# Moving conditioning sums, one copy of normed rows and two gain stores to other quarters in a fused two-block transformer kernel

## The chip, the cores and the metric
The kernel runs as one program on one core of a Trainium2 chip. The metric is the device time of one execution in microseconds (us); the median of three executions of the kernel before is 2072.92 us. Engines are named as in the profile: PE is the matrix engine, DVE and ACT the vector and scalar engines, POOL and SP issue transfers (POOL also copies a little). SP does nothing but issue the weight loads.

## What is computed
Two blocks, one after the other, each on 256 rows of width 1024, all in fp32.

```python
# first block (one layer)
h = h + concat(rms(dilated_attention(...)), rms(moba_attention(...))) @ w_out
h = h + memory_cross_attention(rms(h), rms(mem), w_q_mem, w_kv_mem, w_o_mem)
h = h + conv_ffn(rms(h), w_gate, w_up, conv_w, conv_b, w_down)
# second block, two layers l, streams x and ctx (the context stream only in l = 0)
mod = silu(c) @ ada_w[l] + ada_b[l]          # 6 x 1024 values for x
modc = silu(c_ctx) @ ada_w[l] + ada_b[l]     # 6 x 1024 values for the context
p = (rms(x) * (1 + sc1) + sh1) @ w_in[l]     # q, k, v, gu, gv, conv, gates
y = (ga * (attn @ w_attn_o) + gg * (gmlp @ w_gmlp_o) + gc * (conv @ w_conv_o)) @ w_out[l]
x = x + g1 * rms(y)
x = x + g2 * rms(square(relu(modulate(rms(x), sh2, sc2) @ w_ff1[l])) @ w_ff2[l])
```

The products `silu(c) @ ada_w` are the "conditioning sums": a row times a matrix, done on DVE.

## The kernel before, in words
**Jobs and quarters.** The matrix work is cut into 162 jobs, J0 to J161, each a product of 256 rows with 512 columns of a weight matrix. A job has four quarters ("units"), written J9.2 for quarter 2 of J9. In program order: J0 to J19 are attention and memory attention of the first block (J6 to J8 and J13 weights of the memory's keys and values, J9 to J12 `w_out`, J16 to J19 the output product of the memory attention), J20 to J37 its feed-forward; J38 to J62 the mixer of layer 0 for the context stream, J63 to J87 the same for x (25 jobs later, same order); J88 to J119 the feed-forwards of layer 0; J120 the context's keys and values of layer 1, J121 to J145 its mixer, J146 to J161 its feed-forward. Within the mixer of the context, J38 and J39 are the first half of the conv input, J40 keys and values, J41 and J42 queries, J43 and J44 conv input, J45 to J48 the gmlp inputs, J49 to J58 gates with the attention's and gmlp's output products between (J51, J52 and J55, J56), J59 and J60 the conv's output product, J61 and J62 the last product. The layer norm of the conv sits on J56 to J58.

**How a quarter is done.** SP loads the 512 KB of raw weights into a ring `raw` of 5 buffers (L804); load n is issued once item n-5 of the ring's stream is used up, in order (L793 to L798). ACT copies raw to a rounded `whi` (`split`, L1586) once the load has landed and PE has used the same quarter of the job before. DVE subtracts, giving `wlo` (L2118), and PE does three products per tile (L1189 to L1191, or L1196 to L1198 where the weights move) as soon as `wlo` is there.

**Everything else hangs on quarters.** A function `make_plan` puts steps on a quarter of a job with `put(job, quarter, kind)`. ACT, DVE, PE, POOL and SP each run the steps of their own list strictly in the order of the quarters, so a step that waits holds up all that is behind it on its engine. There is no scheduler: the order is the table and the calls of `put`.

**Conditioning sums.** `COND_AT` (L36 to L38) names one place for each of 96 tiles of `ada_w`: (job, quarter, later), where later = 1 puts it behind the split. At the place DVE runs L1731 over a 128x1024 tile that came through the same ring (load `raw<-ada_wT`, L802) and adds it up to one column of `modc`. For all 48 tiles of layer 0 and the first 16 of layer 1 a second sum, for the context, runs straight behind on the same buffer; such a place is called a pair here.

**Mod steps.** `mod(job, quarter, layer, part, streams)` finishes a part of the modulation. Its "mix gain" part is, for each stream, two small DVE operations on 128x8 (L1820, L1828) and then, on POOL, a store `grow_dram<-modc` (L875) of 4 KB, whose elements of 4 bytes lie apart, with a wait for it before POOL goes on:

```python
pool.dma_start(dst, modc[:, MODS[p.l, p.s], p.first_r:p.units_done],
               allow_slow_non_contiguous=True).then_inc(sem["grow_st"], 16)
pool.wait_ge(sem["grow_st"], 16 * p.k)
```

POOL later loads the gain back as rows (`GB<-grow_dram`, L814).

**Normed rows.** `ynS`, `ynM`, `ynL` make the normed and transposed attention outputs for `w_out` in two halves: `ynM` on DVE is a reciprocal square root (L1785, L1642 to L1649) and a product (L1790), `ynL` copies the result to a rounded high part on ACT (L1340) and a low part on DVE (L1796). Its second half stands on J8.3, the last quarter of a job of the memory's values; J9 and J10 need only the first half, J11 and J12 the second.

Of the kernel before, what the change touches and what calls it, by code (L numbers as in the profile page):

```python
# [32 lines left out]
ON_DVE = ((0, 1, 2), (4, 5))  # L33
RING, LEAD = 5, 2
C2W = 60
COND_AT = (((2, 3, 0), (3, 3, 1), (4, 3, 1), (5, 2, 0), (6, 3, 0), (7, 3, 0), (8, 2, 0), (9, 3, 1), (13, 3, 1), (14, 2, 1), (15, 2, 1), (16, 1, 1), (17, 0, 1), (19, 0, 0), (20, 2, 1), (22, 2, 1), (24, 2, 1), (26, 2, 1), (28, 1, 1), (29, 1, 1), (30, 2, 1), (34, 1, 1), (35, 0, 1), (36, 2, 0), (38, 1, 1), (39, 2, 1), (40, 2, 1), (42, 3, 0), (43, 3, 1), (44, 2, 1), (45, 3, 0), (53, 1, 0), (54, 1, 0), (55, 1, 0), (56, 2, 0), (61, 3, 0), (63, 3, 0), (64, 2, 1), (68, 3, 0), (69, 3, 0), (70, 3, 0), (72, 1, 0), (73, 3, 0), (75, 0, 1), (76, 0, 1), (78, 1, 0), (79, 1, 0), (80, 1, 0)),  # L36
           ((85, 1, 1), (87, 1, 0), (88, 3, 1), (91, 1, 0), (92, 0, 0), (93, 0, 0), (94, 1, 1), (95, 1, 1), (96, 0, 0), (97, 0, 0), (98, 1, 1), (99, 1, 1), (100, 0, 0), (101, 0, 0), (102, 1, 1), (103, 1, 1)),
           ((105, 0, 0), (106, 0, 0), (107, 0, 0), (108, 2, 0), (109, 1, 0), (110, 0, 0), (111, 0, 0), (112, 2, 0), (113, 1, 0), (114, 0, 0), (115, 0, 0), (116, 0, 0), (117, 0, 0), (118, 0, 0), (118, 3, 0), (119, 2, 0), (121, 0, 0), (121, 3, 0), (122, 3, 0), (123, 3, 0), (126, 1, 0), (127, 0, 0), (127, 3, 0), (128, 3, 0), (129, 3, 0), (130, 3, 0), (131, 3, 0), (133, 1, 0), (134, 1, 0), (136, 1, 0), (137, 1, 0), (138, 1, 0)))  # L38
EPS = 1e-6
NEG = -1e30  # L40
MAGIC = 1597463007.0
# [73 lines left out]
def make_plan():  # L115
# [3 lines left out]
    def job(evac, w, n0, typ, slot, k0=0, nk=KT, n=NW, ready=None, **args):  # L119
        units = {8: [[0, 1], [2, 3], [4, 5], [6, 7]], 6: [[0, 1], [2, 3], [4], [5]],  # L120
                 "low": [[0], [1], [2], [3]], "high": [[4], [5], [6], [7]]}[nk]
        jb = Step("job", evac=evac, w=w, n0=n0, typ=typ, slot=slot, k0=k0, nk=nk, cols=n, units=units,
                             ready=ready or {}, aux=[[], [], [], []], **args)
        jobs.append(jb)
        return jb

    def put(jb, q, kind, **args):
        p = Step(kind, **args)
        jb.aux[q].append(p)
        return p  # L130
# [38 lines left out]
    j_vm0 = job("cp", "w_kv", 1024, "A", 1, ready=um, dst=("cres", 0))  # L169
# [14 lines left out]
        put(hosts[2], 1, "ynS", half=group)  # L184
        put(hosts[2], 2, "ynM", half=group)
    put(j_km0, 1, "ynL", slot=2, half=0)
    put(j_vm0, 3, "ynL", slot=2, half=1)
    y_ready = {0: [("yn_lo", None, 0, 1)], 2: [("yn_lo", None, 0, 2)]}
    j_oa = [job("res", "w_out", n * NW, "A", 2, nk="low", ready={0: y_ready[0]}, res="x") for n in range(2)]
    j_ob = [job("res", "w_out", n * NW, "A", 2, nk="high", ready={0: y_ready[2]}, res="x") for n in range(2)]  # L190
    j_vm1 = job("cp", "w_kv", 1536, "A", 1, ready=um, dst=("cres", 1))

    def half_squares(jb, wait_job):
# [50 lines left out]
    def mod(jb, q, l, part, *streams):  # L244

        for s in streams:
            put(jb, q, "mod", l=l, s=s, part=part)
# [196 lines left out]
    t_next = prenorm(d1[1], 2, d2[0], 2, 0, "c", 0, "RA", 0, [("ctx_in", None, 0, 16), ("cp_done", j_q0, 1, 1)])  # L444
    put(d2[1], 1, "gb", src=("g_final",))
    J, co, wo = mixer(0, "c", t_next, (0, 1, 2))
    mod(J["gu0"], 0, 0, "mix gain", "c", "x")

    fin = Step("final", after={"act": [("res_done", d2[1], 1, 1)], "dve": [("res_done", d2[1], 1, 1)]})
    J["ga0"].aux[2].insert(0, fin)  # L450
# [7 lines left out]
    J, _, wo = mixer(0, "x", t_next, (2, 1, 0), tab, first=first)  # L458
# [24 lines left out]
    J, _, wo = mixer(1, "x", t_next, (1, 0, 2), tab, kvc)  # L483
# [12 lines left out]

    places = [at for part in COND_AT for at in part]
    assert places == sorted(places) and len(places) == LAYERS * 6 * KT
# [161 lines left out]

def build(nc, A, out):
    jobs, tail, stream = make_plan()
    with ExitStack() as ctx:
        def tiles3(ap):
# [1537 lines left out]
```

## Time and profile before

| | |
|---|---|
| three executions | 2072.63, 2072.92, 2073.53 us, median 2072.92 |
| the profiled execution | 2073.14 us, span in the profile 2071.3 us |
| granted PE clock, mean | 0.991 of 2.4 GHz |
| busy: PE, DVE, ACT, POOL | 1982.4, 1679.1, 1113.7, 111.5 us |
| what the DMA engines moved | 404.65 MB |

The span is from the first to the last instruction that the profiler saw; the device time is 1.8 us longer. Times inside the trace are counted from the start of the span. An entry of the timeline gives the start, the duration, the engine, the line, what it writes and reads and, in brackets, how long the engine sat idle before it and what ended that. PE is idle for 89 us of the span in all, 17 of them at the start and about 33 at three norms that nothing covers (J19, J145, J161).

### The profile page before, as it was taken

How to read it: one execution, taken by the hardware profiler on the slowest of the kernel's cores; microseconds unless marked ns; L12 is line 12 of the kernel's file. 1: busy time of each engine (PE TensorE's matmuls, PEld its weight loads, DVE VectorE, ACT ScalarE, POOL GpSimd, SP SyncE). 2: the span in 40 equal slices, each digit the busy share in tenths (PEclk: the TensorE clock that was granted, in tenths of full speed). 3: DMA queues.
4: the chain of work that ended last, by engine and by line, in shares of the span. 5: the costliest groups of instructions: out<-in, count | busy, mean ns of one | idle time of the engine just before them, and what ended most of it. 6: DMA issues, size and time to landing. Idle time of an engine off the chain costs nothing.

```text
span 2071.3 us, 29703 instructions
## 1 busy us (share of the span) xinstructions
PE 1982.4 (96%) x11317; PEld 1692.7 (82%) x11317; DVE 1679.1 (81%) x2616; ACT 1113.7 (54%) x1529; POOL 111.5 (5%) x217
## 2 busy tenths in 40 slices
PE   7999979999989999999999999999999999998998
PEld 6877879989878778888777888888888887787886
DVE  5888678888978987988988888977888889876665
ACT  5555444455574365566436654554665664365553
POOL 3000000000004000001300000000000013000000
PEclk9999989999999999999999999999999999999999
DMA  8546466667666655655656667777666566654653
GB/s 264 191 125 205 157 205 204 193 206 250 195 140 202 205 185 191 193 153 177 206 170 192 211 218 247 238 244 239 229 221 197 154 192 204 193 176 130 210 179 121
DMA packets 196718, 404.65 MB, mean 195 GB/s; under 512 B 15815, under 2 KB 18067, under 8 KB 196576
## 3 DMA queue, kind: packets, MB, share of 16 engines
q1 hardware_dynamic: 187888, 387.50, 59.9%
q0 software_dynamic: 8688, 15.25, 2.5%
q8 instruction: 91, 1.49, 0.3%
q14 instruction: 51, 0.42, 0.1%
HBM read 396.74 MB, written 1.10 MB: 192 GB/s over the span
## 4 chain that ended last, share of the span: by engine, by line
PE 73%; DVE 13%; ACT 7%; issue 4%; DMA 2%; DVEq 0%; ACTq 0%
PE gps L1189 13%; PE gps L1191 13%; PE gps L1190 13%; PE gps L1213 8%; PE gps L1196 5%; PE gps L1198 5%; PE gps L1197 5%; PE gps L1215 4%; DVE wlo L2118 3%; ACT whi L1586 2%; PE aps L1125 2%; PE gps L1173 2%; DVE Yc L1934 2%; PE aps L971 1%; PE aps L1097 1%
## 5 line engine op out<-in xcount | busy, mean ns | idle before, releaser
L2118 DVE TENSOR_TENSOR wlo<-raw,whi 128x1024 fp32r<-128x1024 f32 (+1 forms) x648 | 760.2, 1185 | 248.8 <-ACT whi L1586 246.2
L1586 ACT ACTIVATE whi<-raw 128x1024 fp32r<-128x1024 f32 (+1 forms) x648 | 660.4, 1027 | 538.0 <-PE gps L1191 376.8
L1189 PE MATMUL gps<-whi,both 128*128 128x512 f32 x1624 | 649.1, 400 | 9.5 <-DVE wlo L2118 9.5
L1191 PE MATMUL gps<-whi,both 128*128 128x512 f32 x1624 | 634.2, 391 | 0.0
L1190 PE MATMUL gps<-wlo,both 128*128 128x512 f32 x1624 | 633.9, 390 | 0.0
L1189 PEld LDWEIGHTS gps<-whi,both 128*128 128x128 f32 x1624 | 305.8, 188 | 82.7 <-DVE wlo L2118 14.8
L1191 PEld LDWEIGHTS gps<-whi,both 128*128 128x128 f32 x1624 | 305.4, 188 | 65.5
L1190 PEld LDWEIGHTS gps<-wlo,both 128*128 128x128 f32 x1624 | 306.0, 188 | 60.8
L1196 PE MATMUL gps<-both,whi 128*128 128x256 f32 x960 | 276.0, 288 | 2.5 <-DVE wlo L2118 2.5
L1197 PE MATMUL gps<-both,whi 128*128 128x256 f32 x960 | 271.5, 283 | 0.0
L1198 PE MATMUL gps<-both,wlo 128*128 128x256 f32 x960 | 271.5, 283 | 0.0
L1213 PE MATMUL gps<-both,whi 128*128 128x512 f32 x672 | 238.0, 399 | 0.3 <-DVE wlo L2118 0.3
L1731 DVE SCALAR_TENSOR_TENSOR junk<-raw,cond_rows 128x1024 uint8<-128x1024 f32 x160 | 195.1, 1219 | 4.3 <-DMA raw<-ada_wT 3.2
L1196 PEld LDWEIGHTS gps<-both,whi 128*128 128x128 f32 x960 | 183.9, 192 | 8.1 <-issue 4.3
L1934 DVE SCALAR_TENSOR_TENSOR Yc<-GLP,CW,Yc 128x256 f32<-128x256 f32 x450 | 189.0, 478 | 0.0
L1215 PE MATMUL gps<-both,wlo 128*128 128x256 f32 x672 | 188.7, 281 | 0.0
L1197 PEld LDWEIGHTS gps<-both,whi 128*128 128x128 f32 x960 | 184.0, 192 | 0.6
L1198 PEld LDWEIGHTS gps<-both,wlo 128*128 128x128 f32 x960 | 184.0, 192 | 0.0
L1213 PEld LDWEIGHTS gps<-both,whi 128*128 128x128 f32 x672 | 126.3, 188 | 31.9 <-DVE wlo L2118 0.6
L1215 PEld LDWEIGHTS gps<-both,wlo 128*128 128x128 f32 x672 | 127.0, 189 | 0.3
L917 POOL DMA_DIRECT2D QP<-GLP x144 | 70.4, 498 | 77.4 <-PE aps L1073 34.4
L1529 ACT ACTIVATE TT<-gps 128x512 f32<-128x512 f32 x42 | 25.1, 598 | 70.9 <-PE gps L1215 70.9
(306 smaller groups left out, 1746.3 us busy)
## 6 DMA issues: line engine op xcount, KB each, us to landing
raw<-w_in SPq DMA_DIRECT2D x232, 512.0 KB, 4.3
raw<-w_ff SPq DMA_DIRECT2D x192, 512.0 KB, 4.6
raw<-ada_wT SPq DMA_DIRECT2D x96, 512.0 KB, 4.4
raw<-w_attn_o SPq DMA_DIRECT2D x24, 512.0 KB, 4.3
raw<-w_gmlp_o SPq DMA_DIRECT2D x24, 512.0 KB, 4.0
raw<-w_conv_o SPq DMA_DIRECT2D x24, 512.0 KB, 4.3
raw<-w_out SPq DMA_DIRECT2D x24, 512.0 KB, 4.7
raw<-w_gate SPq DMA_DIRECT2D x20, 512.0 KB, 4.6
```

The source lines that it names most:

```text
L1189: mm(om, ah, whi[:, q, i, :], start=first, stop=False)
L1190: mm(om, ah, wlo[:, q, i, :], start=False, stop=False)
L1191: t = mm(om, al, whi[:, q, i, :], start=False, stop=last)
L1196: mm(on, wh, ohi[:, jb.slot, k, :], start=first and n % 2 == 0, stop=False, skip_group_check=True)
L1197: mm(on, wh, olo[:, jb.slot, k, :], start=False, stop=False, skip_group_check=True)
L1198: t = mm(on, wl, ohi[:, jb.slot, k, :], start=False, stop=last, skip_group_check=True)
L1213: mm(tiles(o[:, n * NW:(n + 1) * NW], 2), whi[:, q, i, c], both[:, :, jb.slot, k, :], start=first, stop=False, skip_group_check=True)
L1215: t = mm(o[:, n * NW:n * NW + S], wlo[:, q, i, c], ohi[:, jb.slot, k, :], start=False, stop=last, skip_group_check=True)
L1586: A_(part(whi, jb, q), raw_part(jb, q), ACT.Copy).then_inc(hi_done[q], 1)
L1731: stt(junk[:, :], raw[:, a.at % RING].rearrange("p a n -> p (a n)"), 0.5, CB[:, p.v, :], ALU.mult, ALU.mult, accum_out=modc[:, i, p.r:p.r ...
L1934: stt(y, x, CW[:, p.l, tap * KT + k:tap * KT + k + 1], y, ALU.mult, ALU.add).then_inc(sem["cv_done"], 1)
L2118: tt(part(wlo, jb, q), raw_part(jb, q), f32(part(whi, jb, q)), ALU.subtract).then_inc(lo_done[q], 1)
```

## The change
Three things move; nothing is added or removed in number (96 tiles of sums, one copy, two stores, as before).

1. **Conditioning sums.** `COND_AT` has other places. Taken out (job, quarter, later): (9,3,1), (13,3,1), (14,2,1), (15,2,1), (16,1,1), (17,0,1), (19,0,0), (29,1,1), (36,2,0), (40,2,1), (44,2,1), (45,3,0), (53,1,0), (54,1,0), (55,1,0), (56,2,0), (61,3,0), (78,1,0), (79,1,0), (80,1,0), (85,1,1), (112,2,0), (113,1,0), (122,3,0), (123,3,0), (136,1,0), (137,1,0), (138,1,0). Put in: (14,0,1), (14,3,0), (15,3,0), (29,0,1), (29,3,1), (31,3,1), (40,1,1), (44,3,0), (46,1,0), (47,1,0), (48,3,0), (50,0,1), (50,3,0), (57,1,1), (58,0,1), (58,3,1), (61,0,1), (65,3,0), (71,2,1), (73,0,1), (90,1,0), (112,1,0), (113,0,0), (120,1,0), (122,2,0), (123,1,0), (124,1,0), (125,1,0). The tiles keep their order, so a tile is summed where the next place of the list stands.
2. **The second half of `ynL`** goes from J8.3 to J9.0.
3. **The mix gain of layer 0**, both streams, goes from J47.0 to J41.1.

```diff
@@ COND_AT, first lines of each part @@
-COND_AT = (((2, 3, 0), (3, 3, 1), (4, 3, 1), (5, 2, 0), (6, 3, 0), (7, 3, 0), (8, 2, 0), (9, 3, 1), (13, 3, 1), (14, 2, 1), (15, 2, 1), (16, 1, 1), (17, 0, 1), (19, 0, 0), (20, 2, 1),
...
+COND_AT = (((2, 3, 0), (3, 3, 1), (4, 3, 1), (5, 2, 0), (6, 3, 0), (7, 3, 0), (8, 2, 0), (14, 0, 1), (14, 3, 0), (15, 3, 0), (20, 2, 1),
...
     put(j_km0, 1, "ynL", slot=2, half=0)
-    put(j_vm0, 3, "ynL", slot=2, half=1)
     y_ready = {0: [("yn_lo", None, 0, 1)], 2: [("yn_lo", None, 0, 2)]}
     j_oa = [job("res", "w_out", n * NW, "A", 2, nk="low", ready={0: y_ready[0]}, res="x") for n in range(2)]
     j_ob = [job("res", "w_out", n * NW, "A", 2, nk="high", ready={0: y_ready[2]}, res="x") for n in range(2)]
+    put(j_oa[0], 0, "ynL", slot=2, half=1)
...
     J, co, wo = mixer(0, "c", t_next, (0, 1, 2))
-    mod(J["gu0"], 0, 0, "mix gain", "c", "x")
+    mod(J["q0"], 1, 0, "mix gain", "c", "x")
```

**What the change does to DVE's list at J8 and J9.** `both<-RB,both` is the low part of `ynL`, `wlo` the split of a quarter, `xres<-xres,gps` the evacuation of a job of `w_out`.

```order
 L1790 SCALAR_TENSOR_TENSOR RB<-RB,C,GB 128x256 x4
+L2118 TENSOR_TENSOR wlo<-raw,whi 128x512
 L1796 TENSOR_TENSOR both<-RB,both 128x1024
-L2118 TENSOR_TENSOR wlo<-raw,whi 128x512 x4
-L1731 SCALAR_TENSOR_TENSOR junk,modc<-raw,cond_rows 128x1024
-L1979 TENSOR_TENSOR xres<-xres,gps 128x2x512
-L2118 TENSOR_TENSOR wlo<-raw,whi 128x512
-L1731 SCALAR_TENSOR_TENSOR junk,modc<-raw,cond_rows 128x1024
 L2118 TENSOR_TENSOR wlo<-raw,whi 128x512 x3
```

One split now comes before the low part, and a conditioning sum (two operations) is gone from the quarters behind it.

**DVE's list at J41 and J42**, in the queries of the context; `AB` is the normed keys.

```order
 L1883 TENSOR_TENSOR AB<-AB,st 128x512
 L1851 TENSOR_TENSOR AB<-AB,GQK 128x256 x2
+L1820 TENSOR_TENSOR modc<-modc,ADB 128x8
+L1828 TENSOR_TENSOR modc<-modc,C 128x8
+L1820 TENSOR_TENSOR modc<-modc,ADB 128x8
+L1828 TENSOR_TENSOR modc<-modc,C 128x8
 L2118 TENSOR_TENSOR wlo<-raw,whi 128x1024
 L1934 SCALAR_TENSOR_TENSOR Yc<-GLP,CW,Yc 128x256 x3
```

The four small operations that release the two stores now stand behind the keys' norm, some 85 rows earlier than before.

**POOL's list at the same place.** `GB<-gmlp_norm_g` is a load of the gmlp's gain, `GQK<-k_norm_g` one of the keys' gain.

```order
 L814 DMA GQK<-k_norm_g 128x128
 L814 DMA QP<-gmlp_ws 128x4x128
+L875 DMA grow_dram<-modc 128x8x1 x2
 L814 DMA GB<-gmlp_norm_g 128x1024
-L875 DMA grow_dram<-modc 128x8x1 x2
 L814 DMA GB<-grow_dram 128x1024
```

The two stores pass a load on POOL's queue, which now goes out behind them.

## Rows read from the trace of the kernel before
**Rows 1.** The page: busy time of the engines, and the chain of waits.
```profile
PE 1982.4 (96%) x11317; PEld 1692.7 (82%) x11317; DVE 1679.1 (81%) x2616; ACT 1113.7 (54%) x1529; POOL 111.5 (5%) x217
...
PE 73%; DVE 13%; ACT 7%; issue 4%; DMA 2%; DVEq 0%; ACTq 0%
```
**Rows 2.** Timeline of PE: restarts after idle time, and three rows without one.
```profile
165.31 0.50 PE L1189 MATMUL gps<-whi,both 128*128 128x512 f32 x1 [3.61 <-DVE wlo L2118]
...
167.41 0.63 PE L1190 MATMUL gps<-wlo,both 128*128 128x512 f32 x1
...
463.48 0.50 PE L1189 MATMUL gps<-whi,both 128*128 128x512 f32 x1 [1.16 <-DVE wlo L2118]
...
530.02 1.03 PE L1075 MATMUL aps<-kvb,QP 128*128 128x256 f32 x4
...
617.50 1.10 PE L1097 MATMUL aps<-QP,kvb 128*128 128x256 f32 x4 [2.28 <-ACT QP L1402]
...
763.37 0.50 PE L1189 MATMUL gps<-whi,both 128*128 128x512 f32 x1 [0.82 <-DVE wlo L2118]
...
798.67 0.50 PE L1189 MATMUL gps<-whi,both 128*128 128x512 f32 x1 [1.41 <-DVE wlo L2118]
...
1067.07 1.36 PE L1135 MATMUL aps<-Yc,ones 128*32 128x256 f32 x16 [2.17 <-issue]
...
1127.62 1.09 PE L971 MATMUL aps<-ident,RA 128*128 128x128 f32 x8 [0.92 <-DVE RA L2008]
...
1588.03 0.39 PE L1196 MATMUL gps<-both,whi 128*128 128x256 f32 x1 [0.64 <-DVE wlo L2118]
```
**Rows 3.** Timeline of DVE: the splits behind the low part of `ynL`.
```profile
164.57 2.49 DVE L2118 TENSOR_TENSOR wlo<-raw,whi 128x512 fp32r<-128x512 f32 x4
```
**Rows 4.** Timeline of ACT: the copy at J8, and at J43, J44 and J49.
```profile
162.05 1.06 ACT L1340 ACTIVATE both<-RB 128x1024 fp32r<-128x1024 f32 x1 [6.41 <-DVE RB L1790]
...
525.42 2.16 ACT L1586 ACTIVATE whi<-raw 128x1024 fp32r<-128x1024 f32 x2
527.49 1.01 ACT L1369 ACTIVATE QP<-aps 128x1024 f32<-128x1024 f32 x1
...
615.81 1.06 ACT L1586 ACTIVATE whi<-raw 128x1024 fp32r<-128x1024 f32 x1 [2.11 <-DMA raw<-w_in]
```
**Rows 5.** The page, groups of instructions: the conditioning sums.
```profile
L1731 DVE SCALAR_TENSOR_TENSOR junk<-raw,cond_rows 128x1024 uint8<-128x1024 f32 x160 | 195.1, 1219 | 4.3 <-DMA raw<-ada_wT 3.2
```
**Rows 6.** Busy time per stretch: start, end, length, each engine, PE clock, DMA share, GB/s.
```profile
588.00:618.00 30.00, 25.88 (x116) 20.49 (x115) 22.44 (x42) 19.49 (x34) 2.36 (x3) 1.00 0.68 108
...
592.00:595.00 3.00, 3.00 (x15) 2.47 (x14) 1.25 (x2) 3.00 (x7) 0.00 (x0) 1.00 0.42 17
...
604.00:607.00 3.00, 3.00 (x15) 2.49 (x14) 2.81 (x6) 1.25 (x5) 0.00 (x0) 1.00 1.03 382
...
736.00:764.00 28.00, 26.86 (x117) 21.38 (x116) 22.94 (x35) 21.78 (x28) 1.44 (x2) 1.00 0.49 156
```
**Rows 7.** The store's line, all six of the kernel, min/median/max.
```profile
DMA to landing us min/median/max: 10.3/10.9/13.9
```
**Rows 8.** Timeline of POOL at J47 to J50.
```profile
591.00 0.91 POOL L875 DMA_DIRECT2D grow_dram<-modc  x1 [107.56 <-DVE modc L1828]
601.73 0.89 POOL L875 DMA_DIRECT2D grow_dram<-modc  x1 [9.82 <-DMA grow_dram<-modc]
```
**Rows 9.** DMA issues: whole span; 591.5 to 602; 1080 to 1097. KB each, us to landing.
```profile
raw<-w_in SPq DMA_DIRECT2D x232, 512.0 KB, 4.3
...
raw<-w_in SPq DMA_DIRECT2D x4, 512.0 KB, 14.4
...
raw<-w_conv_o SPq DMA_DIRECT2D x5, 512.0 KB, 12.9
```
**Rows 10.** Timeline of DVE at J41: the row behind which the stores' operations stand.
```profile
510.89 0.76 DVE L1851 TENSOR_TENSOR AB<-AB,GQK 128x256 f32<-128x256 f32 x2
```
**Rows 11.** Timeline of SP: one weight load between the two stores' issues.
```profile
596.65 0.37 SPq L804 DMA_DIRECT2D raw<-w_in  x1
```

More of the change, by code:

```diff
@@ L35 @@
 C2W = 60
-COND_AT = (((2, 3, 0), (3, 3, 1), (4, 3, 1), (5, 2, 0), (6, 3, 0), (7, 3, 0), (8, 2, 0), (9, 3, 1), (13, 3, 1), (14, 2, 1), (15, 2, 1), (16, 1, 1), (17, 0, 1), (19, 0, 0), (20, 2, 1), (22, 2, 1), (24, 2, 1), (26, 2, 1), (28, 1, 1), (29, 1, 1), (30, 2, 1), (34, 1, 1), (35, 0, 1), (36, 2, 0), (38, 1, 1), (39, 2, 1), (40, 2, 1), (42, 3, 0), (43, 3, 1), (44, 2, 1), (45, 3, 0), (53, 1, 0), (54, 1, 0), (55, 1, 0), (56, 2, 0), (61, 3, 0), (63, 3, 0), (64, 2, 1), (68, 3, 0), (69, 3, 0), (70, 3, 0), (72, 1, 0), (73, 3, 0), (75, 0, 1), (76, 0, 1), (78, 1, 0), (79, 1, 0), (80, 1, 0)),
-           ((85, 1, 1), (87, 1, 0), (88, 3, 1), (91, 1, 0), (92, 0, 0), (93, 0, 0), (94, 1, 1), (95, 1, 1), (96, 0, 0), (97, 0, 0), (98, 1, 1), (99, 1, 1), (100, 0, 0), (101, 0, 0), (102, 1, 1), (103, 1, 1)),
-           ((105, 0, 0), (106, 0, 0), (107, 0, 0), (108, 2, 0), (109, 1, 0), (110, 0, 0), (111, 0, 0), (112, 2, 0), (113, 1, 0), (114, 0, 0), (115, 0, 0), (116, 0, 0), (117, 0, 0), (118, 0, 0), (118, 3, 0), (119, 2, 0), (121, 0, 0), (121, 3, 0), (122, 3, 0), (123, 3, 0), (126, 1, 0), (127, 0, 0), (127, 3, 0), (128, 3, 0), (129, 3, 0), (130, 3, 0), (131, 3, 0), (133, 1, 0), (134, 1, 0), (136, 1, 0), (137, 1, 0), (138, 1, 0)))
@@ new lines @@
+COND_AT = (((2, 3, 0), (3, 3, 1), (4, 3, 1), (5, 2, 0), (6, 3, 0), (7, 3, 0), (8, 2, 0), (14, 0, 1), (14, 3, 0), (15, 3, 0), (20, 2, 1), (22, 2, 1), (24, 2, 1), (26, 2, 1), (28, 1, 1), (29, 0, 1), (29, 3, 1), (30, 2, 1), (31, 3, 1), (34, 1, 1), (35, 0, 1), (38, 1, 1), (39, 2, 1), (40, 1, 1), (42, 3, 0), (43, 3, 1), (44, 3, 0), (46, 1, 0), (47, 1, 0), (48, 3, 0), (50, 0, 1), (50, 3, 0), (57, 1, 1), (58, 0, 1), (58, 3, 1), (61, 0, 1), (63, 3, 0), (64, 2, 1), (65, 3, 0), (68, 3, 0), (69, 3, 0), (70, 3, 0), (71, 2, 1), (72, 1, 0), (73, 0, 1), (73, 3, 0), (75, 0, 1), (76, 0, 1)),
+           ((87, 1, 0), (88, 3, 1), (90, 1, 0), (91, 1, 0), (92, 0, 0), (93, 0, 0), (94, 1, 1), (95, 1, 1), (96, 0, 0), (97, 0, 0), (98, 1, 1), (99, 1, 1), (100, 0, 0), (101, 0, 0), (102, 1, 1), (103, 1, 1)),
+           ((105, 0, 0), (106, 0, 0), (107, 0, 0), (108, 2, 0), (109, 1, 0), (110, 0, 0), (111, 0, 0), (112, 1, 0), (113, 0, 0), (114, 0, 0), (115, 0, 0), (116, 0, 0), (117, 0, 0), (118, 0, 0), (118, 3, 0), (119, 2, 0), (120, 1, 0), (121, 0, 0), (121, 3, 0), (122, 2, 0), (123, 1, 0), (124, 1, 0), (125, 1, 0), (126, 1, 0), (127, 0, 0), (127, 3, 0), (128, 3, 0), (129, 3, 0), (130, 3, 0), (131, 3, 0), (133, 1, 0), (134, 1, 0)))
```

## The prediction
> **What bounds the kernel.** I read the page first: PE is busy 96% of the span and carries 73% of the chain of waits, DVE 13%, ACT 7% [rows 1]. So PE is the bound, and a change of order can only win or lose in the 89 us in which PE is idle, or in stretches at half clock. Then I went through PE's timeline for its restarts [rows 2]; the brackets say what ended each idle time, mostly DVE's `wlo` or an ACT copy that DVE or a load held up. Then the stretches [rows 6], for how much of DVE is free where sums come or go, and at last the transfers [rows 7 to 9], since each step that moves takes its DMA along.
>
> A sum is 1219 ns of DVE [rows 5], with its small accumulator read 1.25 us; a pair is 2.5 us. Where DVE is ahead of PE, a pair costs and gives nothing.
>
> **The copy of normed rows.** Before, DVE waits for ACT's copy (162.05, 1.06 us), does the low part and then splits at 164.57 [rows 3, 4]; PE restarts at 165.31, 0.74 us behind the split's start, after 3.61 us [rows 2]. With one split ahead of the copy DVE can split at 162.0, when its product is done, and PE restarts near 162.7. That quarter takes PE 1.36 us; the next split stands behind the copy (about 164.4), so PE waits again until about 165.2. Before, PE reached this second quarter at 165.31 + 1.36 = 166.7: **-1.5 us**. Behind the long idle time PE's rows take 0.63 us at 167.41 where 0.39 is normal [rows 2]; that is the 1.2 GHz level, for 3.4 us, half of which is lost. With two shorter gaps in its place I expect it gone: **-1.6 us** (0 if it stays).
>
> **Sums taken out.** At J36.2 a pair stands right before the `wlo` that PE waits for: PE's 1.16 us at 463.48 [rows 2] go: **-1.2**. At J61.3 likewise, 1.41 us at 798.67 [rows 2]: **-1.4**. J85.1 pushes the row behind PE's 0.92 us at 1127.62 [rows 2]: **-0.9**. J53 to J56: DVE waits there for ACT, which waits for PE; **-0.4** at most. J78 to J80: the same **-0.4**, and 2.17 us of idle at 1067.07 [rows 2] are followed by a stretch at 1.2 GHz of the same length as above; slightly earlier work may save it, 0.8 x 1.6 = **-1.3**. J16 to J19: **-0.2**. J9, J13, J29, J45, J136 to J138: DVE is idle beside them, so 0 (cover: the lead of `wlo` over PE; without it 2.5 us each). Together **-5.8**.
>
> **Sums put in.** J57 to J60: three pairs, 7.5 us, into a stretch where DVE is busy 22.94 of 28 us [rows 6], so 5.1 us are free; the rest is late, and PE already waits for `wlo` behind it at 763.37 [rows 2]: **+2.4**. J124 and J125: two single sums (2.5 us) ahead of splits for which PE already waits 0.64 us at 1588.03 [rows 2]: **+2.5**. J65.3, J71.2, J73.0: three pairs between the head norms and copies of x, of which I take a third, **+2.5** (0 to 7.5: DVE has free time there, but not in the norm itself). J61.0: **+0.6**. J31.3: **+0.4**. J48.3, J50.0, J50.3: **+0.5**. J120.1: **+0.2**. J14, J15, J40, J44, J46, J47, J90, J112, J113, J122, J123: 0, covered as above. Together **+9.1**.
>
> **The two stores.** This is the largest term, and the sums are not part of it. A store of 4 KB takes 10.3 to 13.9 us to land [rows 7]; the second goes out at 601.73, once the first has landed [rows 8], and is over some 13.9 us later. While the first is under way, the core moves 17 GB/s between 592 and 595; at 604 to 607 it is 382 [rows 6]. The four weight loads issued between 591.5 and 602 took 14.4 us, where a load takes 4.3; five at another pair of stores took 12.9 [rows 9]. So for some 25 us a weight load is late by 8 to 10 us. The Trainium skill ("DMA: Bandwidth & Descriptors", "Queues, rings and completion order") says that each DMA engine goes round between the queues it has work for, packet by packet; by that two stores of 4 KB would slow the loads by next to nothing, and the stores' term would be -2.0 us instead of what follows. Rows 6 and 9 speak against it.
>
> Before, the ring is full at this time; only one split is late, ACT's at 615.81 by 2.11 us [rows 4], and PE loses 2.28 us at 617.50 [rows 2]. That goes: **-2.0**. After, the stores' operations stand behind the row at 510.89 [rows 10], so the first goes out about 511.7 and the second about 522.4. The loads for J43.3 and J44.0 are issued within 8 us of the first. At J47 the load issued at 596.65 [rows 11], 5.65 us after the first store, is the one that ACT waited for until 615.81 [rows 4]: 24.8 us after the first store, just behind the second. The next one landed within a microsecond of it. Here that is 536 to 537. Their splits stand at 525.42 to 527.6 now [rows 4], and behind them in ACT's list is the copy of the queries at 527.49, for which PE's product at 530.02 waits [rows 2]. With the split at 537 the copy comes at 538 and PE at 539: **+9.0**, and 9 us of idle time bring the 1.2 GHz level, which at 167.41 cost up to 1.6: **+1.0**. Bounds: +1 if J44.0 is the only thing late and lands with the first two (14 to 16 us after the first store), +12 if the second store's 13.9 us apply. The load `GB<-gmlp_norm_g`, which the stores pass on POOL's queue, has 60 us left: 0. Together **+8.0**.
>
> **The sum.** -3.1 - 5.8 + 9.1 + 8.0 = +8.2 us. Against the profiled execution's 2073.14 (span 2071.3 and 1.8 around it; the median of the three is 0.2 lower) that is **2081.3 us**. Changes within 0.2% (4.1 us) can't be told from none here: faster is below 2068.8, slower above 2077.1.
>
> **Rivals.**
> - *The loads slip past the stores* (the other side). Place: J43.3 and J44.0; it decides whether these two loads land before about 527, ahead of the second store, as four of the five did at 1080 to 1097 (they were issued within 10.4 us of the first store and landed by 16.6 us after it). Then nothing is late at J43, and all the idle time of PE in 588 to 618, 30 - 25.88 = 4.1 us [rows 6], goes with the stores. The stores' term is -4.1 instead of +8.0: 2069.2 us. Against it: at J47 the same spacing of loads was caught. The skill's rule on the queues would lead here too. 0.28.
> - *The sums put in are absorbed.* DVE's free time at J57 to J60 and J65 to J73 lies where it is needed, and at J124 PE's lead takes it: 8.0 of the 9.1 us go: 2073.3 us. For it: DVE is free for 19% of the span [rows 1]. Against: the steps in front of these splits are chains, which can't be moved into the gaps. 0.16; with the first rival as well, 2061.2: 0.08.
> - *The copy does not do what it says.* ACT, not DVE, sets J9: the evacuation moved ahead of the copy waits for PE, so the copy is late and J11 waits for it. The 3.1 us stay: 2084.4. 0.05.
>
> **How the numbers follow.** Forecast 0.43, the rivals 0.28, 0.16, 0.08 and 0.05. Around each stand some 3 us for the unknown sizes. Slower by over 0.2%: most of the forecast, the last rival and a little of the third: 0.45. Faster by over 0.2%: half of the first rival, the double case and a little: 0.25. Within: 0.30. The range leaves out the double case and the upper end of the stores' bound: 2066 to 2085; the forecast's own is 2077 to 2085.
>
> **What the profile after would show.** Stores of L875 near 512 and 523; ACT's split near 537 after 8 to 9 us of waiting for `raw<-w_in`; PE's L1075 restarting near 537 after some 9 us; no 2.28 us at J49; PE near 162.7 at J9 and no row of 0.63 us behind; DVE without a gap from 736 to 764 and PE waiting 2 us more there and at J126. I am wrong if ACT waits under 2 us at J43 and J44, or if PE's idle times at J60, J68 and J126 are as before.

## The result and the profile after

The changed kernel takes 2085.02 us (median of four executions, 2081.78 to 2086.65) where the kernel before took 2072.78 beside it (2072.24 to 2073.53). The ratio is 1.0056, 95% interval 1.0044 to 1.0069: 9 to 14 us slower. The profiled execution is the longest of the four (2086.65 us, span 2084.8, mean PE clock 0.985 against 0.991); the shortest, 2081.78, ran at a mean clock of 0.990. Of the executions below, one of `mods_only` that took 4011 us is left out of every number.

The page of the changed kernel, to be set against [rows 1]:

```profile
span 2084.8 us, 29701 instructions
...
PE 1991.6 (96%) x11317; PEld 1700.3 (82%) x11317; DVE 1678.5 (81%) x2616; ACT 1114.3 (53%) x1529; POOL 111.7 (5%) x217
...
PE 71%; DVE 15%; ACT 7%; issue 4%; DMA 2%; DVEq 0%; ACTq 0%
```

The same matmuls are busy 9 us longer (1991.6 against 1982.4), and PE is idle 93 us against 89. So in these two executions only about a third of the difference is waiting; the rest is work at the lower clock level (1.2 GHz), which by the mean clocks lasts some 63 us in all against 37. Not all of that belongs to the change, as shown further down.

PE's waits of the changed kernel, what it waited for, total, times, longest:

```profile
PE aps L971 <- DVE RB L1676: 19.8, 3, 10.0
...
PE aps L1075 <- ACT QP L1369: 8.7, 1, 8.7
PE gps L1189 <- DVE wlo L2118: 8.2, 11, 2.4
PE gps L1196 <- DVE wlo L2118: 4.7, 3, 2.4
```

The 8.7 us are new: before, this product ran at 530.02 without a wait [rows 2]. Timeline of POOL, then of ACT, then of PE in the changed kernel, at the mix gain's new place:

```profile
503.53 0.91 POOL L875 DMA_DIRECT2D grow_dram<-modc  x1 [257.23 <-DVE modc L1828]
514.71 0.89 POOL L875 DMA_DIRECT2D grow_dram<-modc  x1 [10.27 <-DMA grow_dram<-modc]
```
```profile
516.91 1.06 ACT L1586 ACTIVATE whi<-raw 128x1024 fp32r<-128x1024 f32 x1 [6.02 <-DMA raw<-w_in]
...
528.34 1.06 ACT L1586 ACTIVATE whi<-raw 128x1024 fp32r<-128x1024 f32 x1 [7.61 <-DMA raw<-w_in]
529.30 1.01 ACT L1369 ACTIVATE QP<-aps 128x1024 f32<-128x1024 f32 x1
```
```profile
530.45 2.05 PE L1075 MATMUL aps<-kvb,QP 128*128 128x256 f32 x4 [8.67 <-ACT QP L1369]
```

It reads as the forecast had it for J44.0: its load is in only at 528.34, 24.8 us after the first store was issued, ACT's split of it waits 7.6 us, the queries' copy stands behind the split, and PE stands 8.67 us. The load for J43.3 was not late with it: ACT splits it at 519.68, about 16 us after the first store, before the second can hold it up. The program is by then some 8 us ahead of the kernel before, so the times are earlier than forecast by that much.

Stretches of the changed kernel (columns as in [rows 6]); the clock is the third number from the end:

```profile
526.00:534.00 8.00, 3.55 (x12) 3.22 (x13) 3.94 (x6) 2.91 (x3) 0.56 (x1) 0.50 0.90 303
722.00:730.00 8.00, 7.72 (x38) 5.89 (x39) 3.37 (x4) 1.45 (x2) 0.00 (x0) 0.79 0.51 170
752.00:766.00 14.00, 11.12 (x41) 8.35 (x40) 11.46 (x13) 10.84 (x14) 0.00 (x0) 0.88 0.62 223
1598.00:1606.00 8.00, 6.51 (x35) 6.24 (x36) 6.75 (x9) 3.10 (x4) 0.00 (x0) 0.79 0.78 243
```

Behind the stall at J43 (until 535.9, and once more at 546 to 550), in the layer norm, at J59 and at J126 the clock is down for some microseconds; in the stretches that answer to these four the kernel before has a clock of 1.00. The fall in the layer norm can't be put down to the change, though: `copy_only` (0.58 over 718 to 722) and `j19_only` (0.57 over 720 to 724) below have it as well, and they leave the sums there and the stores alone.

The other places, PE's restarts of the changed kernel, against [rows 2]:

```profile
161.76 0.50 PE L1189 MATMUL gps<-whi,both 128*128 128x512 f32 x1 [0.97 <-DVE wlo L2118]
...
164.18 0.50 PE L1189 MATMUL gps<-whi,both 128*128 128x512 f32 x1 [0.77 <-DVE wlo L2118]
...
760.71 0.50 PE L1189 MATMUL gps<-whi,both 128*128 128x512 f32 x1 [2.37 <-DVE wlo L2118]
...
1127.13 1.09 PE L971 MATMUL aps<-ident,RA 128*128 128x128 f32 x8 [0.30 <-DVE RA L2008]
...
1599.49 0.38 PE L1196 MATMUL gps<-both,whi 128*128 128x256 f32 x1 [2.39 <-DVE wlo L2118]
```

The one wait of 3.61 us at J9 has become two of 0.97 and 0.77, and no matmul behind them takes 0.63 us. J59 has a wait of 2.37 us, J126 one of 2.39 where it was 0.64.

Where each quarter starts in the one and in the other tells where the difference of the two profiled executions (13.5 us at the end) comes from: -3.2 at J9 and J10, -2.9 at J20, -1.9 at J37, +12.9 at J43 and J44, -2.2 at J49, +1.0 at J51, +6.5 from J56 to J60, +0.7 and -1.8 at J61 and J62, +3.2 from J67 to J74, -1.8 at J85 and J86, +4.1 at J125 and J126 (the rest is in steps under 1 us).

### The profile page after: what moved, and what is told of

Read it like the earlier page. It is cut to its first block, busy times and chain, and to the rows that moved or that the text cites. A ratio compares the mean times of both kernels' runs of the same rounds, so it can differ in the third digit from the quotient of the medians.

```text
span 2084.8 us, 29701 instructions
## 1 busy us (share of the span) xinstructions
PE 1991.6 (96%) x11317; PEld 1700.3 (82%) x11317; DVE 1678.5 (81%) x2616; ACT 1114.3 (53%) x1529; POOL 111.7 (5%) x217
## 4 chain that ended last, share of the span: by engine, by line
PE 71%; DVE 15%; ACT 7%; issue 4%; DMA 2%; DVEq 0%; ACTq 0%
PE gps L1189 12%; PE gps L1191 12%; PE gps L1190 12%; PE gps L1213 8%; PE gps L1196 5%; PE gps L1198 5%; PE gps L1197 5%; DVE wlo L2118 4%; PE gps L1215 4%; ACT whi L1586 2%; DVE Yc L1934 2%; PE aps L1125 2%; PE gps L1173 1%; PE aps L971 1%; DVE junk L1731 1%
## 5 line engine op out<-in xcount | busy, mean ns | idle before, releaser
L1196 PEld LDWEIGHTS gps<-both,whi 128*128 128x128 f32 x960 | 186.7, 194 | 10.7 <-DVE wlo L2118 5.4
L1197 PEld LDWEIGHTS gps<-both,whi 128*128 128x128 f32 x960 | 186.7, 195 | 0.7
L1213 PEld LDWEIGHTS gps<-both,whi 128*128 128x128 f32 x672 | 126.3, 188 | 31.9 <-DVE wlo L2118 0.6
```

The source lines that it names most:

```text
L1196: mm(on, wh, ohi[:, jb.slot, k, :], start=first and n % 2 == 0, stop=False, skip_group_check=True)
L1197: mm(on, wh, olo[:, jb.slot, k, :], start=False, stop=False, skip_group_check=True)
L1213: mm(tiles(o[:, n * NW:(n + 1) * NW], 2), whi[:, q, i, c], both[:, :, jb.slot, k, :], start=first, stop=False, skip_group_check=True)
```

## The experiments

All ratios are to the kernel before, run on the same chip in the same rounds, with 95% intervals; a thousandth is 2.07 us. The difference of two ratios is uncertain by some 3 us. Each profile is of one execution.

### Are the stores the cause?

`mods_back`: the change, with the mix gain back.

```diff
-    mod(J["q0"], 1, 0, "mix gain", "c", "x")
+    mod(J["gu0"], 0, 0, "mix gain", "c", "x")
```

> The change with the mix gain of layer 0 back on J47.0, everything else as in the change. Theory (the two gain stores hold up the loads for J43.3 and J44.0): the 8.7 us that PE waits for the queries' copy and the half clock behind it go, the 2.2 us at J49 come back, so 2085.0 - 11 = about 2074 us. Rival (the sums and the copy make the loss, the stores only happen to sit there): it stays above 2082 us.

Measured: 1.0023 (1.0013 to 1.0034), median 2077.54: neither the 2074 of the theory nor the 2082 of the rival. So the stores' place is worth more than half of the loss, but not all: the sums and the copy are 4.8 us slower without it, which leads to the table of sums.

`mods_only`: the kernel before, with the mix gain alone moved.

```diff
-    mod(J["gu0"], 0, 0, "mix gain", "c", "x")
+    mod(J["q0"], 1, 0, "mix gain", "c", "x")
```

> The kernel before with the mix gain alone moved to J41.1. Theory of the stores: slower than before by 9 to 12 us, about 2083 us, with PE idle 8 to 9 us at J43 or J44 behind the copy of the queries. Rival (the stores hurt only because the changed kernel has less lead there, from the sums at J40 and J44): under 4 us slower, below 2077 us.

Measured: 1.0047 (1.0033 to 1.0061), 9.7 us slower (median of five 2083.74). PE's waits of this kernel have the same new row, and the rival (less lead through the moved sums) falls:

```profile
PE aps L1075 <- ACT QP L1369: 9.6, 1, 9.6
```

### One store or two?

`one_store`: the kernel before, the context's store early, the x stream's where it was.

```diff
+    mod(J["q0"], 1, 0, "mix gain", "c")
+    mod(J["gu0"], 0, 0, "mix gain", "x")
-    mod(J["gu0"], 0, 0, "mix gain", "c", "x")
```

> The kernel before with only the context's mix gain on J41.1 and the x stream's left on J47.0, so one store goes early. Theory (it is the second store, started as soon as the first has landed, that catches the loads of J43.3 and J44.0): these loads land about 5 us after the single store has, by 528, and PE waits under 3 us there: at most 3 us slower than before, and the stall at J49 of before gets smaller, so 2071 to 2076 us. Rival (one store is enough): half or more of the loss of the two, 2078 us or more.

Measured: 1.0023 (1.0013 to 1.0032), 4.8 us slower, median 2077.76: half of what the two cost, so nearly the rival's case and not the theory's. ACT and PE in this kernel (its lines are numbered one higher):

```profile
526.27 1.06 ACT L1587 ACTIVATE whi<-raw 128x1024 fp32r<-128x1024 f32 x1 [6.71 <-DMA raw<-w_in]
...
532.27 1.06 ACT L1587 ACTIVATE whi<-raw 128x1024 fp32r<-128x1024 f32 x1 [1.42 <-DMA raw<-w_in]
```
```profile
534.38 2.04 PE L1076 MATMUL aps<-kvb,QP 128*128 128x256 f32 x4 [3.94 <-ACT QP L1370]
```

One store holds back the loads for about 12 us; the splits then follow each other at the pace at which the loads land, not at ACT's, and PE waits 3.94 us, with the clock low until 540.3. I had put under 3 us on it, since I counted only one late load and not the queue of them. The second store makes up the other half: with it the same load is late by another store's time.

### Is it the 4 KB or the pieces?

`runs_32b`: the kernel before with the mix gain at J41.1, and the destination laid out in runs. The rows of the gain come out in another order by this, so the kernel computes something else; the work is the same.

```diff
-dst = grow_dram.ap()[...].rearrange("(r c) -> c r", c=P)
+dst = grow_dram.ap()[...].rearrange("(c r) -> c r", c=P)
```

> The kernel before with the mix gain moved to J41.1, and the store's destination laid out so that the 8 values of a partition lie together (runs of 32 bytes, 128 of them, where it was 1024 single values of 4 bytes); the gain rows are permuted by this, so the output is another. Theory (the count of scattered pieces is what takes the 10 us and holds up the loads, not the 4 KB): a store lands in about 2 to 3 us, the loads in their usual 4 to 5 us, no stall at J43, and the stall at J49 gone: 2069 to 2072 us. Rival (any store by POOL to memory in this place costs as much): landing 10 us and about 2083 us as with the scattered form.

Measured: 0.9984 (0.9974 to 0.9993), 3.3 us faster than before, median 2069.55. The store's line, all six of this kernel, against [rows 7]:

```profile
DMA to landing us min/median/max: 1.7/3.0/4.0
```

Same bytes, same place, same queue, 128 pieces for 1024: 3.0 us for 10.9, no stall at J43, and 13 us between this kernel and `mods_only` (0.9984 and 1.0047). So the cause is the scattered form, and the place only decides how much of it shows. In `runs_32b` J49 starts its second quarter 2.2 us earlier than before, and J85 and J86 some 2 us. Of these about half can't be put down to the stores: in `copy_only`, which keeps them as they were, the two places are 1.0 and 1.4 us earlier too. Whether a scattered store issued by another engine would do the same was not tried.

### The sums and the copy, each alone

`sums_only`: the kernel before with the changed `COND_AT`.

> The kernel before with the changed table of sums alone; the copy and the mix gain stay where they were. By the trace of the change the table gains 2.6 us at J20 (the pair at J19.0 gone), 1.9 at J37, 1.8 at J62, 1.8 at J85 and J86, and loses 5 to 6 at J58 to J60, 3 at J67 to J74, 4 at J125 and J126, 1 at J51 and 0.7 at J61. Theory (the table is a net loss): 5 to 8 us slower than before, 2078 to 2081 us. Rival (the places gain as much as they lose, as the sum of the prediction had it, +3.3): 2074 to 2077 us.

Measured: 1.0036 (1.0025 to 1.0047), 7.5 us slower, median 2081.18. The table is a net loss, twice as large as predicted. Some 4 us of it arise at J49 to J51, where the whole change loses 1.0. ACT and PE of `sums_only` there:

```profile
610.61 1.06 ACT L1586 ACTIVATE whi<-raw 128x1024 fp32r<-128x1024 f32 x1 [5.44 <-DMA raw<-w_in]
611.57 0.89 ACT L1394 ACTIVATE QP<-QP,den 128x256 f32<-128x256 f32 x2
```
```profile
612.61 1.09 PE L1084 MATMUL aps<-ident,QP 128*128 128x128 f32 x4 [5.06 <-ACT QP L1394]
```

In the kernel before, this product at 611.85 waits 1.65 us. It is the stores again, at their old place J47.0: with the added sums around them a late load meets a step that PE needs sooner, and the mean clock over 610 to 618 is 0.57. `mods_back` and `combined_slow` have the same (waits of 3.98 and 3.90 us); `combined_fast`, which has these sums and short stores at J47.0, has not (1.31 us). Which of the added sums does it was not tried.

`copy_only`: the kernel before with `put(j_oa[0], 0, "ynL", slot=2, half=1)` in place of `put(j_vm0, 3, ...)`.

> The kernel before with the second half of the copy moved to J9.0 and nothing else. Theory (one split ahead of the copy and no half clock behind a shorter wait): PE restarts near 162.7 and stays at full clock, 3 us faster, about 2069.5 us. Rival (the conditioning sum at J9.3, which this kernel keeps, or the clock takes it back): under 1.5 us faster.

Measured: 0.9989 (0.9978 to 0.9999), 2.3 us faster, median 2070.93, with PE's restarts at 162.02 and 164.45 and full clock behind. The low level behind J9's long wait is in each of the seven profiles that keep the copy at J8.3 and in none of the seven that have it at J9.0. J9 and J10 gain 3.2 us in this profile, but PE gives 1.2 back at 188.50, in a wait of 1.35 us for normed rows that neither the kernel before nor the changed one has. The three parts alone, 9.7 + 7.5 - 2.3 = 14.9 us, are some 4 us uncertain and so agree with the whole change's 9 to 14; they need not add up, since the loss at J49 in `sums_only` needs the stores at J47.0.

### Which sums?

`ln_sums_out`: `mods_back` with three pairs moved out of the layer norm's quarters. Not both sums of a place with later = 1 stand behind the split: `make_plan` puts the context's sum on the next quarter, and the first sum stays in front. So these three places are six single sums in front of six quarters, and a tile keeps its place in the ring until the second of them (737.15 and 746.46 in the profile of the change for J57.1). J53 to J55 are true pairs.

```diff
-(57, 1, 1), (58, 0, 1), (58, 3, 1),
+(53, 1, 0), (54, 1, 0), (55, 1, 0),
```

> The change with the mix gain back on J47.0 and the three pairs at J57.1, J58.0 and J58.3 back on J53.1, J54.1 and J55.1. Theory (these pairs stand in front of the layer norm's chain and of splits that have no lead, so nearly each of their 7.5 us shows): 5 us less than the same kernel with them (2077.5), about 2072.5 us, and PE's waits of 2.4 us at J59 gone. Rival (DVE's 5 us of free time there take them, as the prediction had it): 2 to 3 us less, 2075 us.

Measured: 0.9999 (0.9989 to 1.0008), against 1.0023 with them: 5.0 us for the three pairs, 2 to 8 by the intervals (median 2073.48). In the two profiles the quarters from J56 to J61 differ by 5.5 us. The stretch 744 to 772 of this kernel, and of the change, which is some 6 us behind it there:

```profile
744.00:772.00 28.00, 26.84 (x121) 21.45 (x120) 23.39 (x30) 20.04 (x26) 0.00 (x0) 1.00 0.63 204
```
```profile
744.00:772.00 28.00, 23.88 (x95) 18.27 (x93) 24.26 (x36) 19.98 (x26) 1.44 (x2) 0.94 0.46 161
```

DVE is free for more than 3 us in both, and PE does 3 us less of work in the second, with a part of the stretch at the lower clock. DVE's timeline of the change says why the free time does not help:

```profile
754.04 1.23 DVE L2118 TENSOR_TENSOR wlo<-raw,whi 128x1024 fp32r<-128x1024 f32 x1
757.03 1.22 DVE L1955 SCALAR_TENSOR_TENSOR RB<-RB,Yc 128x1024 f32<-128x1024 f32 x1 [1.76 <-ACT RB L1455]
758.17 1.22 DVE L1731 SCALAR_TENSOR_TENSOR junk<-raw,cond_rows 128x1024 uint8<-128x1024 f32 x1
```

DVE sits idle for 1.76 us in the layer norm, for ACT's tanh, and then has the sum to do before the split that PE waits for at 760.71. DVE's step and the split are both in order behind what came before: DVE's free time lies where ACT is late, and the sum where DVE is.

`j19_only`: the kernel before with one pair moved, `(19, 0, 0)` to `(15, 3, 0)`.

> The kernel before with the one pair at J19.0 put on J15.3 instead (the tiles between shift by a place). The prediction gave its removal nothing. Theory (DVE and the load of this pair stand in the chain of the norm at J19 and J20, which nothing covers; DVE waits 3.2 us for it at 259.3): PE's wait at the norm falls from 12.5 to about 10 us, 2 to 3 us faster than before, about 2070.5 us. Rival (nothing, as predicted: the norm is set by PE and ACT): within 1 us of before.

Measured: 0.9989 (0.9980 to 0.9999), 2.3 us faster (0.2 to 4.1), median 2071.98. In the profile the longest wait for the norm's rows falls only from 12.51 to 11.4 us. The prediction's "nothing" is wrong; how much it is for this pair alone, 1 or 2 us, stays open.

`combined_slow` and `combined_fast`: `ln_sums_out` with five more of the added sums back where they were, and, in the second, the short store with a result that is still the reference's.

```diff
-(65, 3, 0), (71, 2, 1), (73, 0, 1), (124, 1, 0), (125, 1, 0)
+(78, 1, 0), (79, 1, 0), (80, 1, 0), (136, 1, 0), (137, 1, 0)
```
```diff
+G = GB[:].rearrange("p (c r) -> p r c", r=D // P)[:, jb.j * NW // P:(jb.j + 1) * NW // P, :]
+rc = lambda t: t.rearrange("p (r c) -> p r c", c=P)
-tt(y[:, 1, j], src[:, 1, :], GB[:, j], ALU.mult)
+tt(rc(y[:, 1, j]), rc(src[:, 1, :]), G, ALU.mult)
... (the other three products likewise)
```

> The combined table, copy and place of the mix gain, with the scattered stores as in the kernel before. Against the same with ln_sums alone moved back (2073.3) it tells what the sums at J65.3, J71.2, J73.0, J124.1 and J125.1 cost: theory 3 + 3 to 4 us, so 2067 us; rival (PE's lead had absorbed them): 2071 us or more. Against the combined kernel with short stores (2065.5) it tells what these give: 2 to 4 us.

> What the runs so far favour, put together: the change's copy and the sums it takes out at J9 to J19, J36, J61 and J85; the sums that it puts in at J57, J58, J65, J71, J73, J124 and J125 at J53 to J55, J78 to J80, J136 and J137 instead, as before; the mix gain on J47.0; and the store in runs of 32 bytes, with the gain's rows read through a strided view so that the result is that of the reference. Theory (each cause is local, so the terms add): 2077.5 - 5 (J57, J58) - 3 (J65 to J73) - 3 (J124, J125) - 3 (stores) = about 2063.5 us, faster than both kernels. Rival (the gains run into each other, or the strided view costs DVE time at the two gained evacuations): 2068 us or more.

Measured: 0.9969 (0.9957 to 0.9981), median 2067.08, and 0.9962 (0.9949 to 0.9976), median 2066.24. Both beat both kernels, by 6 and 8 us against before. Against `ln_sums_out` the five places (three pairs, two single sums, 10 us of DVE) cost 0.9999 - 0.9969, 6.2 us; in the profiles it is 3.0 at J65 to J74 and 3.3 at J124 to J126. The short store with its view gave 1 us on top, which is within the noise; 2 to 4 were expected. In the profiles it gives 3.8 us at J49 and loses most of it again further on.

`fast_store`: the kernel before with only that store and view. `after_fast`: the whole change with them.

> The kernel before with the gain stores in runs of 32 bytes and the strided view of the gain's rows, all else in place, the output as the reference's. Theory: a store lands in about 3 us; PE's 2.3 us at J49 go and some 2 us at J85 and J86, so 3 to 4 us faster than before, about 2069.5 us. Rival (the strided view costs what the stores give): within 1 us of before.

> The whole change, mix gain on J41.1, but with the stores in runs of 32 bytes. Theory (the place of the stores is harmless once they are short, and the sums and the copy stay as they are): the change's 2084.5 less 11.5 for the stall and less some 1.5 at J85, about 2073 us, no stall at J43. Rival (at J41 any store or the load behind it on POOL's queue does harm): 2077 us or more.

Measured: `fast_store` 1.0013 (1.0003 to 1.0022), 2.7 us slower than before, outside the theory and the rival; `after_fast` 1.0006 (0.9996 to 1.0015), median 2074.9, near the 2073 expected, with no stall at J43. The stores land in 2.8 and 3.1 us (medians), so they did their part. In the profile of `fast_store` the quarters behind J49 and J86 are 2.8 us ahead of before, and all of it is lost again by J121. What most likely took it back is the view. The gained evacuation (L2054 before, L2056 here) in `fast_store`, then in the kernel before:

```profile
L2056 DVE TENSOR_TENSOR RB<-gps,GB 128x512 f32<-128x512 f32 x6 | 6.7, 1111 | 0.9 <-PE gps L1191 0.9
```
```profile
L2054 DVE TENSOR_TENSOR RB<-gps,GB 128x512 f32<-128x512 f32 x6 | 4.1, 689 | 0.9 <-PE gps L1191 0.9
```

Reading one operand with a step of 32 bytes takes 1111 ns for 689. There are 24 of these, 10 us of DVE in all, and they stand in the chains ahead of the norms: between `runs_32b`, which has the same store and no view, and `fast_store` lie 6 us (0.9984 and 1.0013). The two differ also in the mix gain's place, so the view alone is not isolated. A version that reads the rows in one run and still stores in runs was not tried.

## Why the prediction was right, and where it was not

The forecast was 2081.3 us (+8.2), the measurement 2085.0 (+12.2 to the median, 9 to 14 by the ratio). That is at the very top of the stated range of 2066 to 2085. Direction, place and mechanism of the largest term held; the table of sums was put at under half of what it cost, so the range held the result only at its edge.

- **The two stores, +8.0.** Right in mechanism: the row that ACT waits for, the copy behind it, PE's product behind that, 24.8 us from the first store to the late load, as at J47, 8.67 us of idle time for the 9.0 forecast. `mods_only` gives 9.7 us. Mis-sized was the clock behind the stall: I put 1.0 us. In the profile PE works at 1.2 GHz from 530.45 to 535.9, 5.4 us and not the 3.4 of J9, which loses 2.7, and another 1.5 are lost at 546 to 550: 8.7 + 2.7 + 1.5 is the 12.9 us by which J44's last quarters are late. The fall at 546 comes and goes (it is in `mods_back`, `sums_only` and `j19_only` too, without the stall), so it can't be put down to the stores alone.
- **The rival that the loads slip past, 0.28.** Half of its condition came true in the change: J43.3 slipped past, J44.0 did not. In `mods_only` both were late (ACT waits 2.83 and 4.46 us for them). PE stood behind the late split in both kernels, so the rival's time was never reached. The Trainium skill ("DMA: Bandwidth & Descriptors", "Queues, rings and completion order") says that a DMA engine goes round the queues it has work for, packet by packet. Whether it does so here no run shows, but it did not keep the loads from being late: the 21 weight loads issued beside the six scattered stores of the kernel before took 6 to 19 us, median 11.2, and the five beside the stores of `runs_32b` 3.7 to 6.4.
- **The copy, -3.1.** Right: 161.76 and 164.18 where I had 162.7 and 165.2, the program being 1 us ahead there, and no time at 1.2 GHz behind. Alone it measured -2.3.
- **Sums taken out, -5.8.** J36 (-1.9 in the profile for -1.2), J61 (-1.8 for -1.4) and J85 (-1.0 for -0.9) were right or a little low. The other 0.8 at J85 is no effect of this pair: a wait of 0.84 us at 1111.91 is gone, and it is gone in `copy_only` and `j19_only` too, which keep the pair. J19.0 was costed at nothing, with the norm's chain as set by others; `j19_only` shows 2.3 us. Before, DVE waits 3.2 us for that pair's weights at 259.3, and since the pair holds a place of the ring, ACT waits 7.49 us for the load of its next split at 262.63; in `j19_only` that wait is 5.40 us and in the change, where the other pairs from J13 on have moved too, 4.78. DVE would have waited there for ACT anyhow (5.76 us for the next split in `j19_only`), so it was the place in the ring more than DVE's time that the pair cost, before a norm that nothing covers. The 1.3 us for the clock at J81 did not come in the change; in `mods_back` and `sums_only`, with the same sums, it did, so it is a matter of the single execution.
- **Sums put in, +9.1.** The step that failed is J57 to J60: "5.1 us are free; the rest is late". DVE's free time in a stretch was set against the new work as if it could be moved. I expected DVE without a gap from 736 to 764; it still had 2.9 us of gaps there, and PE waited all the same. Against J53 to J55 the three pairs cost 5.0 us by `ln_sums_out`, where the forecast has 2.4 and takes off 0.4 for leaving J53 to J56: 2.0. J65 to J73 with J124 and J125 cost 6.2 us against their old places, for 5.0 less 0.4 and 1.3 for J78 to J80: 3.3. What is left, the copy and the rest of the table, is `combined_slow`: -6.4 measured, -5.1 forecast. So the added sums in front of splits without lead cost twice the forecast, and the rest held.
- Together the table was +3.3 forecast and +7.5 measured alone, of which some 4 are at J49 and need the stores at J47.0; stores 8.0 and 9.7; copy -3.1 and -2.3.

## To carry to other kernels

A small store in single elements can cost more than a large load: look up its time to landing, then what else was in flight, and give it runs, or put it where no load is needed for the next 15 to 25 us. Where every engine runs its list in order, free time of an engine in a stretch is no room for work: what counts is the lead of the next instruction that someone waits for, and behind a chain that alternates between two engines it is none. A wait of PE of 2 us and more should be costed with a clock term of its own and with its spread: it was 2.7 us behind the wait of 8.7, 3.0 behind the 3.9 of `one_store`, 1.5 behind the 2.4 of J59, and nothing behind the 2.28 at 617.50 of the kernel before. And work that moves through a ring costs its place there too, not only the engine that uses it.

## What the runs showed of the hardware

- **Pieces.** 4 KB stored as 1024 pieces of 4 bytes take 10.9 us, and the 512 KB weight loads issued meanwhile take 11.2 us (median of 21) for 4.3; the core moves 17 GB/s between 592 and 595 where it moves 382 at 604 to 607 [rows 6]. As 128 pieces of 32 bytes they take 3.0 us, and five loads beside them took 3.7 to 6.4 us.
- **Stepped reads on DVE.** A 128x512 fp32 product with one operand at a step of 32 bytes takes 1111 ns for 689 (`fast_store` against the kernel before).
- **The clock as noise.** The four executions of the change lie 4.9 us apart, 2081.78 at a mean clock of 0.990 and 2086.65 at 0.985. 0.5% of 2085 us is 10.4 us of full speed, of which PE loses only what falls on its work: enough for the whole spread. Over all 108 executions of the 13 changed kernels, each set against its own kernel's mean, a mean clock lower by 0.001 goes with a time longer by about 1.2 us (an estimate by a straight line). So a kernel's single profile says where a wait is, but not what its clock term is worth.
